# Feed forward's down projection as seven block products, and the conditioning rows in the input projection

## The reference, cut to what matters

```python
u = rmsnorm(x, g_mix) @ w_in            # 1024 tokens x 1024, first block
...                                     # four mixers, merged, w_out
h2 = rmsnorm(x, g_mlp)
x = x + square(relu(h2 @ w_ff1)) @ w_ff2        # 1024 -> 4096 -> 1024
x = x + (p @ w_ple) * sigmoid(rmsnorm(x, g_ple) @ w_ple_gate)
x = rmsnorm(x, g_final)
# second block, on that x
mod   = (silu(c)     @ w_ada + b_ada)   # six rows of 1024, used for x
mod_c = (silu(c_ctx) @ w_ada + b_ada)   # the same for ctx; only rows 0 and 1 are used
...
```

## Time and profile before

| | |
|---|---|
| Median of 3 runs | 3533.78 us (3532.81 to 3534.66) |
| The profiled execution | 3534.49 us, its span 3532.7 us |
| TensorE busy, mean granted clock | 3403.0 us, 0.987 |
| VectorE, ScalarE, GpSimd busy | 2259.5, 1575.2, 799.2 us |
| Input projection with attention | from about 57 us |
| Feed forward up, down | about 1256 to 1576, 1576 to 1921 us |

### The profile page before, as it was taken

The page is one execution under the profiler, slowest core; times in us unless marked ns, Lnnn a source line. Parts: engine busy times, 40 slices in busy tenths (PEclk is TensorE's granted clock), DMA queues, the critical chain, the costliest instruction groups (busy, mean ns, idle before and its releaser), DMA issues.

```text
span 3532.7 us, 43926 instructions
## 1 busy us (share of the span) xinstructions
PE 3403.0 (96%) x17289; PEld 2803.6 (79%) x17289; DVE 2259.5 (64%) x2915; ACT 1575.2 (45%) x1946; POOL 799.2 (23%) x396
## 2 busy tenths in 40 slices
PE   7999999999999999999999999999896999999998
PEld 6667767667878878888888877777775999999997
DVE  4333445645447675666764854545756899999998
ACT  4344443234322343332213433433545677777776
POOL 3111111112212345544431221111222011101112
PEclk9999999999999999999999999999998999999999
DMA  5111113223465323336542241232633999999998
GB/s 201 49 48 54 66 54 103 78 96 131 160 216 184 101 87 117 117 137 223 203 158 71 81 158 65 81 119 98 191 124 151 389 379 378 388 385 385 380 379 311
DMA packets 131725, 626.75 MB, mean 177 GB/s; under 512 B 14849, under 2 KB 15241, under 8 KB 106690
## 3 DMA queue, kind: packets, MB, share of 16 engines
q1 hardware_dynamic: 126626, 606.12, 46.1%
q0 software_dynamic: 4752, 17.30, 1.8%
q10 hardware_dynamic: 144, 0.52, 0.0%
HBM read 520.67 MB, written 103.19 MB: 177 GB/s over the span
## 4 chain that ended last, share of the span: by engine, by line
PE 55%; DVE 6%; ACT 1%; issue 1%; DMA 1%; POOL 0%; POOLq 0%; DVEq 0%; SPq 0%; ACTq 0%
PE bank L268 8%; PE bank L270 7%; PE bank L269 7%; PE bank L3870 5%; PE bank L3869 5%; PE bank L3868 5%; PE bank L2123 3%; PE bank L2125 3%; PE bank L2124 3%; PE bank L3884 2%; PE bank L3885 2%; PE bank L3886 2%; DVE gqJ L2975 1%; PE bank L3855 1%; PE bank L2849 1%
## 5 line engine op out<-in xcount | busy, mean ns | idle before, releaser
L257 POOL TENSOR_TENSOR WL<-WR,WH 128x1024 fp32r<-128x1024 f32 (+1 forms) x177 | 400.6, 2263 | 1721.6 <-ACT WH L249 1718.5
L268 PE MATMUL bank<-XH,WH 128*128 128x512 f32 x1584 | 637.5, 402 | 10.0 <-ACT stg L553 5.0
L270 PE MATMUL bank<-XH,WL 128*128 128x512 f32 x1584 | 617.9, 390 | 0.0
L269 PE MATMUL bank<-XL,WH 128*128 128x512 f32 x1584 | 617.6, 390 | 0.0
L249 ACT ACTIVATE WH<-WR 128x1024 fp32r<-128x1024 f32 (+1 forms) x177 | 173.4, 979 | 511.4 <-PE bank L270 506.3
L3804 DVE TENSOR_TENSOR EL<-ER,EH 128x2816 fp32r<-128x2816 f32 x120 | 371.3, 3100 | 2.2 <-POOL warm L4095 2.2
L268 PEld LDWEIGHTS bank<-XH,WH 128*128 128x128 f32 x1584 | 297.8, 188 | 88.7 <-issue 15.9
L3799 ACT ACTIVATE EH<-ER 128x2816 fp32r<-128x2816 f32 x120 | 307.5, 2563 | 117.2 <-PE bank L3870 84.4
L269 PEld LDWEIGHTS bank<-XL,WH 128*128 128x128 f32 x1584 | 298.1, 188 | 64.7 <-issue 5.0
L270 PEld LDWEIGHTS bank<-XH,WL 128*128 128x128 f32 x1584 | 297.7, 188 | 62.9
L3868 PE MATMUL bank<-EH,WH 128*128 128x352 f32 x1024 | 336.2, 328 | 1.9 <-DVE WL L3992 1.9
(11 more groups left out here) (655 smaller groups left out, 6956.5 us busy)
## 6 DMA issues: line engine op xcount, KB each, us to landing
ER<-in_wu_dram SPq DMA_DIRECT2D x48, 1408.0 KB, 8.6
ER<-in_wd_dram SPq DMA_DIRECT2D x40, 1408.0 KB, 10.9
WR<-in_w_in_dram SPq DMA_DIRECT2D x89, 512.0 KB, 4.4
ER<-in_wg_dram SPq DMA_DIRECT2D x32, 1408.0 KB, 8.5
WR<-in_w_ff_dram SPq DMA_DIRECT2D x64, 512.0 KB, 4.7
aq<-in_w_ada_dram SPq DMA_DIRECT2D x48, 512.0 KB, 3.6
res<-in_wg_dram SPq DMA_DIRECT2D x16, 1408.0 KB, 8.0
res<-in_wu_dram SPq DMA_DIRECT2D x16, 1408.0 KB, 8.3
```

Source lines behind the costliest of these rows:

```text
L257: e.tensor_tensor(lo, raw, hi.bitcast(F32), ALU.subtract).then_inc(*w_lo.up("w_lo", n))
L268: e.matmul(bank[bk][:, 0:b - a], whi, xhi, start=k == 0, stop=False)
L269: e.matmul(bank[bk][:, 0:b - a], whi, xlo, start=False, stop=False)
L270: mm = e.matmul(bank[bk][:, 0:b - a], wlo, xhi, start=False, stop=k == K - 1)
```

## The change

**Down projection.** The seven factors are no longer built from blocks after a plain reload: `up_factor` makes the four T factors on VectorE in the up projection (T1 = C12 - C11, T3 = C22 - C12, T2 = C22 - T1, T4 = T2 - C21), and `D_f` holds seven factors of four chunks. SP stores seven blocks a unit instead of four. The down projection is units 16 to 31: chunk c = n // 4 - 4, two blocks of the residual each, weights in the form of `up_load`/`up_sum`/`up_hi`/`up_lo`. TensorE's order is products 0 to 3 of unit n, then 4 to 6 of unit n - 1; unit 16 has only its four. Results go to eight banks in turn, six from unit 28 on. Product 0 is copied to SBUF by ScalarE (`keep_first`); VectorE adds products 1, 2 (twice), 4 and 6 to the residual and makes the two kept sums with 3 and 5; GpSimd adds the kept values (`first_back`, `second_back`, `third_back`), four additions of 128 x 512 a unit. A chunk's factors come in seven loads of 1 MB, each as its old contents have been used for the last time; ScalarE makes the high parts, VectorE the low parts in two halves of 128 x 1024, but for factor 2 of the first chunk, which GpSimd makes. Weights of products 4 and 5 get a second slot, in `stg`. The sums of squares, high and low parts for the next stage lie in the last units, and its first tile takes half 1 before half 0.

**Conditioning rows.** They move to the input projection, with both operands in SBUF and 1024 columns at once; the context's half is made for the first 16 blocks only: 64 instructions. The diagonals and sixteen broadcast matmuls come behind tile 0, ScalarE copies the result to SBUF. Rows 0 to 21 lie behind tiles 0 to 4 in five groups, rows 22 to 31 in the chain of norms, 32 to 37 between rotary products, 38 to 47 behind them. SP loads them through three, then four slots.

The diff, cut to its core:

```diff
+    ADA_EARLY, ADA_CHAIN, ADA_LATE = ((0, 3), (3, 7), (7, 11), (11, 15), (15, 22)), ((22, 25), (25, 29), (29, 32)), 38
+    d_ada = [dma_sem("ada0"), dma_sem("ada1"), d_p, *d_x]
+    ada_b, ada_junk, ada_diag = (qk[:, 3 * T:4 * T], qk[:, 0:T]), qk[:, 2 * T:3 * T], mcs
+
+    def ada_slot(a):
...
+    def ada_load(e, a):
+        if a >= ADA_LATE + 4:
+            e.wait_ge(*on("ada.ev", a - 4, 0))
+        elif a >= ADA_LATE:
+            e.wait_ge(*(on("mla.qr", 1, 1, 1) if a == ADA_LATE else on("mla.kr")))
+        elif a >= 3:
+            e.wait_ge(*on("ada.ev", a - 3, 1 if a - 3 < 16 else 0))
+        e.dma_start(ada_raw(a), I["w_ada"][a]).then_inc(*d_ada[ada_slot(a)].up("ada", a))
...
+    def ada_pe(e):
+        for i in range(2):
+            e.wait_ge(*on("ada.diag", i))
+            for h in range(2):
+                e.wait_ge(*on.bank(4 + 2 * i + h, "ada.b", i, h))
+                for k in range(4):
+                    o = i * T + (4 * h + k) * 128
+                    mm = e.matmul(bank[4 + 2 * i + h][:, k * 128:k * 128 + 128], ones, ada_diag[:, o:o + 128],
+                                  start=True, stop=True)
+                mm.then_inc(*mla_pe.up("ada.bc", i, h))
...
+    def ada_rows(e, a, b):
+        for x in range(a, b):
+            e.wait_ge(*on("ada", x))
+            for i in range(2 if x < 16 else 1):
+                if x == 0:
+                    for k in range(12, 16):
+                        e.wait_ge(*on("p.out", k))
+                    for h in range(2):
+                        e.wait_ge(*on("ada.b", i, h))
+                e.wait_ge(*mla_dve.now)
+                e.tensor_tensor_reduce(ada_junk, ada_raw(x), ada_b[i], 1.0, pr("b_ada", x), ALU.mult, ALU.add,
+                                       mod[:, x, i:i + 1]).then_inc(*mla_dve.up("ada.ev", x, i))
...
     def attention_pe(e, st):
+        for k in range(5):
+            st.until(2 * k + 2, "ada", k)
+            if k == 0:
+                ada_pe(e)
         st.until(12, "a0")
...
+            ada_rows(e, *ADA_CHAIN[s])
...
+        ada_rows(e, *ADA_CHAIN[2])
...
+        ada_rows(e, ADA_LATE, 48)
+        on.at["ada.end",] = mla_dve.now
...
+    def up_factor(e, n, i):
+        if i == T1:
+            for b in (C11, C12):
+                e.wait_ge(*on("up.sq", n, b))
+            if n:
+                e.wait_ge(*on("h.out", n - 1, T1))
+            a, b = c_slots[C12], c_slots[C11]
+        elif i == T3:
+            e.wait_ge(*on("up.sq", n, C22))
+            e.wait_ge(*on("ff.T", n, T1))
+            a, b = c_slots[C22], c_slots[C12]
+        elif i == T2:
+            if n:
+                e.wait_ge(*on("h.out", n - 1, T4))
+            a, b = c_slots[C22], T_AT[T1]
+        else:
+            e.wait_ge(*on("up.sq", n, C21))
+            e.wait_ge(*on("h.out", n, T2))
+            a, b = T_AT[T2], c_slots[C21]
+        e.tensor_tensor(T_AT[i], a, b, ALU.subtract).then_inc(*ff_dve.up("ff.T", n, i))
...
+    def down_load(e, c, i):
+        e.wait_ge(*on("up.mm", 15 + 4 * c, i))
+        for n in range(4 * c, 4 * c + 4):
+            e.wait_ge(*on("h.out", n, i))
+        e.dma_start(factor4(i, False), D_f[c, i].rearrange("p (a b) -> p a b", b=512)).then_inc(*d_fin[i].up("f.in", c, i))
+
+    def down_hi(e, c, i):
+        e.wait_ge(*on("f.in", c, i))
+        for s in range(2):
+            e.activation(factor4(i, True, s), factor4(i, False, s), AF.Copy).then_inc(*ff_act.up("f.hi", c, i, s))
+
+    def down_lo(e, by, c, i):
+        for s in range(2):
+            e.wait_ge(*on("f.hi", c, i, s))
+            e.tensor_tensor(factor4_lo(i, s), factor4(i, False, s), factor4(i, True, s).bitcast(F32),
+                            ALU.subtract).then_inc(*by.up("f.lo", c, i, s))
+
+    def up_store(e, n, i):
...
+        for n in range(16, 33):
+            if n < 32:
+                for i in range(4):
+                    unit_pe(e, n, i)
+            if n > 16:
+                for i in range(4, 7):
+                    unit_pe(e, n - 1, i)
+        for h in range(2):
+            on.holder[6 + h] = "ff.q_free", 14 + h
...
+        p_ = {i: bank[dn_bank(n - lag(i), i)][:, :] for i in range(7) if 16 <= n - lag(i) < 32}
+        first_, last, before = n < 32 and first_of_chunk(n), last_of_chunk(n), n > 16 and first_of_chunk(n - 1)
+
+        def r(u, t, h):
+            return xc(u % 4 * 2 + t)[:, half(h)]
+
+        def next_los(*mh):
+            for m, h in mh:
+                next_lo(e, V, "ple", "g_ple", m, h)
+
+        def sums(i):
+            if n < 31:
+                up_sum(e, n + 1, i)
+
+        if first_:
+            down_lo(e, V, n // 4 - 4, 3)
+        if n == 31:
+            ff_sq_dve(e, (2, 0), (2, 1))
+        if n < 32:
+            e.wait_ge(*on("up.mm", n, 1))
+            e.tensor_tensor(r(n, 0, 0), r(n, 0, 0), p_[1], ALU.add).then_inc(*V.up("dn.p2", n))
+            if n == 16:
+                up_factor(e, 15, T3)
+                up_factor(e, 15, T2)
+            e.wait_ge(*on("up.mm", n, 2))
+            e.tensor_tensor(r(n, 0, 1), r(n, 0, 1), p_[2], ALU.add).then_inc(*V.up())
+            e.tensor_tensor(r(n, 1, 1), r(n, 1, 1), p_[2], ALU.add).then_inc(*V.up("dn.p5", n))
+            sums(2)
+            if before:
+                if n > 17:
+                    down_lo(e, V, n // 4 - 4, 4)
+                else:
+                    down_lo(e, V, 0, 5)
+            if n == 30:
+                ff_sq_dve(e, (1, 0), (1, 1))
+            if n == 31:
+                ff_sq_dve(e, (3, 0), (3, 1))
+                next_los((0, 0), (0, 1), (1, 0))
+            e.wait_ge(*on("up.mm", n, 3))
+            e.wait_ge(*on("dn.p1", n))
+            if n > 17:
+                e.wait_ge(*on("dn.r12", n - 2))
+            else:
+                e.wait_ge(*(on("up.lo", 16, 5) if n == 16 else on("h.out", 15, T3)))
+            e.tensor_tensor(keep2[n % 2], p_[3], keep1, ALU.add).then_inc(*V.up("dn.p6", n))
+            sums(3)
+            if n == 16:
+                up_factor(e, 15, T4)
+                down_lo(e, V, 0, 4)
+        if before:
+            if n > 17:
+                down_lo(e, V, n // 4 - 4, 5)
+            else:
+                down_lo(e, V, 0, 6)
+        if last:
+            down_lo(e, V, n // 4 - 3, 0)
+        if n == 31:
+            next_los((1, 1), (2, 0), (2, 1))
+        if n == 32:
+            ff_sq_dve(e, (4, 1))
+            next_los((4, 1))
+        if n > 16:
+            u = n - 1
+            e.wait_ge(*on("up.mm", u, 4))
+            e.wait_ge(*on("dn.r12", u))
+            e.tensor_tensor(r(u, 0, 1), r(u, 0, 1), p_[4], ALU.add).then_inc(*V.up("dn.p3", u))
+            on.at["ff.res", u % 4 * 2, 1] = on.at["dn.p3", u]
+        sums(4)
+        if n > 17 and before:
+            down_lo(e, V, n // 4 - 4, 6)
+        if last:
+            down_lo(e, V, n // 4 - 3, 1)
+        if n == 31:
+            next_los((3, 0), (3, 1))
+            ff_sq_dve(e, (4, 0))
+        if n == 32:
+            next_los((5, 1))
+            ff_sq_dve(e, (5, 1))
+        if n > 16:
+            e.wait_ge(*on("up.mm", u, 5))
+            e.wait_ge(*on("dn.p6", u))
+            if u > 16:
+                e.wait_ge(*on("dn.r21", u - 1))
+            else:
+                e.wait_ge(*on("h.out", 15, B21))
+                e.wait_ge(*on("ff.T", 15, T4))
+            e.tensor_tensor(keep3, p_[5], keep2[u % 2], ALU.add).then_inc(*V.up("dn.p7", u))
+        sums(5)
+        if last:
+            down_lo(e, V, n // 4 - 3, 2)
+        if n == 31:
+            next_los((4, 0))
...
+        for n in range(16, 31):
+            up_lo(e, n + 1, 0)
+            up_lo(e, n + 1, 1)
+            first_back(e, n)
+            up_lo(e, n + 1, 2)
+            second_back(e, n)
+            up_lo(e, n + 1, 3)
+            up_lo(e, n + 1, 4)
+            third_back(e, n - 1, 1)
+            up_lo(e, n + 1, 5)
+            third_back(e, n - 1, 0)
+            up_lo(e, n + 1, 6)
+        first_back(e, 31)
```

More of the change, by code:

```diff
@@ new lines, in ada_act, with ada_diag_dve @@
+    def ada_act(e):
+        for i in range(12, 16):
+            e.wait_ge(*on("p.out", i))
+        for i in range(2):
+            for h in range(2):
+                e.wait_ge(*on("ada.bc", i, h))
+                e.activation(ada_b[i][:, half(h)], bank[4 + 2 * i + h][:, :], AF.Copy).then_inc(
+                    *mla_act.up("ada.b", i, h))
+    def ada_diag_dve(e):
+        e.wait_ge(*on("a0.cv"))
+        for i in range(2):
+            for k in range(8):
+                o = i * T + k * 128
+                e.tensor_scalar(ada_diag[:, o:o + 128], ident, cf[:, 2 * k + i:2 * k + i + 1], None,
+                                ALU.mult).then_inc(*mla_dve.up("ada.diag", i))
```

566 lines of the change are left out of this document (354 added, 212 removed).

## The result

After: 3570.34 us (median of 4, 3564.54 to 3571.14); before, on the same chip: 3534.21 (3532.81 to 3534.66). The ratio is 1.0099, with a 95% interval of 1.0082 to 1.0117: the change made the kernel slower by some 36 us, where 9 were forecast and the range ended at 3562. The profiled execution of after took 3564.54 us, 6 less than the other three; in it 30.0 us of the difference can be followed (span 3562.7 against 3532.7).

The account below looks back on a forecast made before the run. TensorE was taken as the bound, busy 3403.0 of 3532.7 us. Savings -51.1, input projection +26, chunk changes +24, first chunk +10, tail +1 gave +9.9 on 3533.8: 3543 us; own range 3530 to 3562, overall 3503 to 3562.

Parts of the forecast that it names:

- The signs by which the forecast was to be known as wrong: Forecast wrong if the input projection's angle starts before 128 us, or the chunk-changing units' waits sum to under 20 us.
- Matmuls removed: Down projection: 1536 matmuls become 1344, 192 fewer at 0.2267 us each, -43.5 us, all on the path.
- Input projection, +26: Conditioning rows on VectorE there delay TensorE by 26 us, 3.7 of it moved broadcasts; bounds +12 to +32.
- Its delay passes on whole: Input projection: the angle chain, already 1.27 us late, starts at about 137 and passes its whole delay on: +24 us.
- Up projection, 0: Four more subtractions and three more stores a unit cost nothing, eight banks giving a full unit of slack.
- Changes of chunk: Down projection: replacing the seven factors every fourth unit makes TensorE wait 8 us at each of three changes, +24.
- The walk's second part: Chunk change: GpSimd's late last low part delays weights and the weight sum ahead of factors 4 to 6: +6.9 us.
- The sign by which it was to be known: Chunk changes: VectorE's low halves take 2 to 2.4 us, not 1.22, with waits of 8 to 10 us each.
- First chunk, +10: Start of down projection: unit 16's four products leave little time for factor work, ScalarE running late: 10 us, from 6 to 14.
- Tail, +1: End of down projection: next gain and block 7's low parts come within 1 us of need: +1 (0 to 4).
- Rival (b): Port-bound down projection, delay carried over the chunk, input projection at +30: +40 us, 3574; chance 0.07.
- Rival (a): Port sharing costs little in input and down projection: -25 us, 3509, faster; chance 0.40.

Follow-up runs that it names:

- e4: Changed kernel with conditioning row group five moved from ahead of the angle chain into its gaps and behind: 3575.97 us, ratio 1.0115.
- e12: Changed kernel with GpSimd's low parts of the weights of input projection tiles 3 to 8 cut to 8 of 1024 columns: 3557.06 us, ratio 1.0058.
- e3: Changed kernel, from unit 19 GpSimd's low parts for products 0, 1, 6 and its additions back cut to 8 of 512 columns: 3544.30 us, ratio 1.0029.
- e13: Changed kernel, from unit 19 only GpSimd's four additions back cut to 8 of 512 columns, low parts whole: 3552.55 us, ratio 1.0043.
- e15: e3 with additions back cut from unit 16 and low parts of weights 0 and 1 from unit 17: 3545.11 us, ratio 1.0030.
- e8: Changed kernel, ScalarE in step 16 makes factor 6's high halves behind those of unit 17's weights 2 and 3: 3570.39 us, ratio 1.0097.
- e1: Changed kernel, VectorE in units 21, 25, 29 makes factor 4's low halves ahead of the next unit's first weight sum: 3565.98 us, ratio 1.0087.
- e7: Changed kernel, GpSimd in steps 20, 24, 28 makes product 6's weight low part ahead of those of 4 and 5: 3565.97 us, ratio 1.0090.
- e10: Changed kernel, bank 1 evicted by ScalarE instead of VectorE in input projection tiles 1 to 5: 3570.93 us, ratio 1.0098.
- e6: Changed kernel with the four additions back to the residual of each unit on VectorE instead of GpSimd: 3575.43 us, ratio 1.0114.

## Why the prediction was wrong

Its sign was right and its size was not. The step that failed is a term put at nothing without a reason: the half clock behind the new waits. Beside it, the waits in the input projection were put too high and those of the first chunk too low. The signs by which the forecast was to be known as wrong (the angle before 128, waits in the changing units under 20 us) did not come, since neither looks at the clock. Step by step, by the profiled executions:

- **Matmuls removed, -43.5, broadcasts moved, -3.7:** held; 1344 x 0.2267 = 304.7, and 304.7 + 41.8 of waits + 14.6 of half clock = 361.1 of the stage's 361.8.
- **Input projection, +26:** 26.4 measured, but not by the walk. Groups ended at 76.6, 93.1, 106.5, 119.8 and 134.0 (forecast 77.1, 93.2, 107, 121, 136.5) and the diagonals were waited for 4.5 us (4): so far right, ports and all. The waits for bank 1 were 0.3, 2.2, 2.2 and 0.9 (forecast 11 in all), then came 4.0 and 5.0 behind the angle chain: 16.0 us more of waits than before, 3.7 of broadcasts and 6.8 of half clock. The total agreed by luck: a term that the sum hadn't, the clock, stood in for waits that didn't come. "Its delay passes on whole" was wrong as a mechanism: e4 and e12 start the angle equally early, and one gains nothing, the other 9 us.
- **Up projection, 0:** held (1.5 less, half clock).
- **Changes of chunk, 3 x 8 = +24:** 22.5 measured, and that they come from GpSimd's work beside VectorE's held in e3 and e13. The walk's second part was right in kind, the weight sum ahead of factor 4. The sign by which it was to be known was only half there: VectorE's 54 low halves have medians of 1.47 (YL) and 1.22 us (XL), not 2 to 2.4. But 23 of them were held, up to 2.3 us. That GpSimd's late start and the load that it releases cost more than the held instructions is my reading of the timeline, and no run shows it.
- **First chunk, +10:** 16.4, mis-sized, and its cause stays open (e15, e8). The walk had ScalarE 2 to 3 us late for unit 17's third weight; the wait there was 4.2, and nine others stand around it.
- **Tail, +1:** 2.7.
- **The missing term:** 14.6 us of half clock in the down projection. The sum counts every wait once, and I used a clock drop as an upper bound for the input projection alone. The trace of the kernel before had the price in it, behind the longest wait between 57 and 1926 us, at the start of the up projection (the wait, then the stretch):

```profile
1271.34 0.80 PE L2123 MATMUL bank<-XH,WH 128*128 128x512 f32 x1 [3.87 <-DVE XL L1996]
...
1271.00:1278.00 7.00, 6.66 (x17) 5.14 (x18) 5.46 (x6) 3.06 (x6) 3.18 (x2) 0.59 0.20 62
```

  The clock lost 3.4 us there; behind its two other waits of over 2 us (3.0 and 2.2) it lost nothing.

  With 14.6 the sum of 9.9 becomes 24.5; the first chunk adds 6.4 and the tail 1.7; the changes of chunk and the up projection take off 1.5 each, and some tenths elsewhere give 0.4 back: 30.0. Without any half clock the difference is 30.0 - 13.7 - 6.8 + 1.7 = 11.2, near the 9.9, again with terms that make up for each other: the input projection's waits and broadcasts were 19.7 us, not 26, and the down projection's waits 41.8, not the 35 of the sum.
- The other 6 us of the medians lie in executions without a trace. Their clocks were 0.980 to 0.981 where the profiled one had 0.982, and 0.001 of 3563 us is 3.6: half clocks again, by inference.

Rival (b) came nearest in time (3574 against 3570) and was wrong in kind: it put 43.5 + 14 + 4 = 61.5 us into waits in the down projection where 41.8 were, and the clock made up the most of the rest. Rival (a) needed waits under 15 us there, or under 29 with a cheaper input projection.

Of the two pages weighed in the prediction, the Trainium skill's GPSIMD Engine Reference, section Specifications, is the one that the runs bear out: a reduction with two SBUF inputs took 3.29 us beside GpSimd and 1.28 without it (e12).

## What to carry to other kernels

Hold a saving on the bound engine against every stretch in which its feeders are nearly full, counted together where two of them share a port: there a reordering moved the waits about and gained 3 us of the stage at most (e1, e4, e7, e8, e10), and moving work from the slower to the faster feeder gained nothing (e6). When a change adds waits of some microseconds to TensorE, add a term for the half clock behind them: here 20.5 us beside 55.6 us of listed waits. And when a forecast's total agrees, look whether its terms do.
